# Memory feed-forward up projection: rounded features and remainders in one 512-column matmul, the two halves of the bank summed by ScalarE and VectorE

## The reference

```python
def swiglu(h, w_in, w_out):
    g, u = _split(h @ w_in, (D_FF, D_FF))
    return (jax.nn.silu(g) * u) @ w_out
...
        x = x + swiglu(rms_norm(x, norm_ffn[i]), ffn_w_in[i], ffn_w_out[i])
```

## Time and profile before

| | before |
|---|---|
| device time, median of 3 runs | 1661.8 us (1661.35 to 1661.95) |
| profiled execution: span from first to last instruction | 1659.6 us |
| its own time, with what lies around the span | not listed apart; the median lies 2.2 us over the span |
| granted TensorE clock, mean of the span | 0.998 of full |
| TensorE matmuls busy | 98% of the span |
| VectorE, ScalarE, GpSimd busy | 66%, 54%, 25% |
| DMA | 160 GB/s on average |

### The profile page before, as it was taken

How to read it: one execution, slowest core, us unless ns; L and a number is a source line. 1 busy time by engine, 2 the same in 40 slices (tenths; PEclk the granted TensorE clock), 3 DMA queues, 4 the chain that set the end, 5 groups by cost and what they waited for, 6 DMA issues and landing times. The chain is left out here.

```text
span 1659.6 us, 26949 instructions
## 1 busy us (share of the span) xinstructions
PE 1619.1 (98%) x10929; PEld 1462.8 (88%) x10929; DVE 1096.3 (66%) x1546; ACT 891.3 (54%) x1401; POOL 421.5 (25%) x460
## 2 busy tenths in 40 slices
PE   8999999999999999999999999999999999999999
PEld 7767899987887889998889998999888999999997
DVE  6875665645576665655577768777646876867763
ACT  6465554434455555443456746566445684756652
POOL 2500100002341120000147802244204690214430
PEclk9999999999999999999999999999999999999999
DMA  7523376556330236665555444766556444376652
GB/s 278 174 77 101 103 205 194 185 197 213 99 135 27 77 102 172 185 186 193 174 195 164 147 133 147 189 185 190 181 154 220 159 153 130 131 204 187 190 179 76
DMA packets 287067, 265.30 MB, mean 160 GB/s; under 512 B 12256, under 2 KB 247520, under 8 KB 286944
## 3 DMA queue, kind: packets, MB, share of 16 engines
q1 hardware_dynamic: 286944, 263.59, 50.8%
HBM read 262.52 MB, written 1.05 MB: 159 GB/s over the span
## 5 line engine op out<-in xcount | busy, mean ns | idle before, releaser
L144 DVE TENSOR_TENSOR w_lo<-w_raw,w_hi 128x2048 fp32r<-128x2048 f32 (+2 forms) x244 | 565.8, 2321 | 288.6 <-ACT w_hi L143 283.6
L143 ACT ACTIVATE w_hi<-w_raw 128x2048 fp32r<-128x2048 f32 (+2 forms) x244 | 462.9, 1902 | 214.6 <-PE bank L529 125.5
L1873 PE MATMUL bank<-h_hi,w_hi 128*128 128x256 f32 x1984 | 565.5, 285 | 4.7 <-issue 1.2
L1874 PE MATMUL bank<-h_lo,w_hi 128*128 128x256 f32 x1984 | 561.3, 283 | 0.0
L1875 PE MATMUL bank<-h_hi,w_lo 128*128 128x256 f32 x1984 | 561.2, 283 | 0.0
L1873 PEld LDWEIGHTS bank<-h_hi,w_hi 128*128 128x128 f32 x1984 | 380.5, 192 | 8.2 <-issue 7.5
L1874 PEld LDWEIGHTS bank<-h_lo,w_hi 128*128 128x128 f32 x1984 | 380.7, 192 | 0.1
L1875 PEld LDWEIGHTS bank<-h_hi,w_lo 128*128 128x128 f32 x1984 | 380.6, 192 | 0.0
L456 PE MATMUL bank<-w_hi,h_hi 128*128 128x512 f32 (+1 forms) x288 | 113.4, 394 | 5.4 <-DVE w_lo L144 3.3
L2953 POOL TENSOR_TENSOR cffn_hidden<-cffn_conv 128x256 f32<-128x256 f32 x44 | 73.7, 1675 | 155.5 <-ACT cffn_conv L2984 155.5
L457 PE MATMUL bank<-w_lo,h_hi 128*128 128x512 f32 (+1 forms) x288 | 111.9, 388 | 0.0
(11 more groups left out here) (447 smaller groups left out, 2858.0 us busy)
## 6 DMA issues: line engine op xcount, KB each, us to landing
w_raw<-in_w_in SPq DMA_DIRECT2D x48, 1024.0 KB, 5.0
w_raw<-in_ffn_w_in SPq DMA_DIRECT2D x88, 512.0 KB, 5.0
w_raw<-in_w_up SPq DMA_DIRECT2D x88, 512.0 KB, 5.2
w_raw<-in_ffn_w_out SPq DMA_DIRECT2D x22, 1024.0 KB, 4.9
w_raw<-in_w_down SPq DMA_DIRECT2D x22, 1024.0 KB, 5.0
w_raw<-in_nsa_w_in SPq DMA_DIRECT2D x10, 1024.0 KB, 5.2
w_raw<-in_mem_w_kv SPq DMA_DIRECT2D x8, 1024.0 KB, 5.1
w_raw<-in_w_branch SPq DMA_DIRECT2D x8, 1024.0 KB, 5.1
```

The costliest lines, as they stand in the source:

```text
L143: return act.activation(hi, raw, ACT.Copy)
L144: return dve.tensor_tensor(self.lo[:, cut_slot, 0:k * n], raw, hi.bitcast(F32), ALU.subtract)
L1873: pe.matmul(out, h, hi[:, f, :], start=(f == 0), stop=False)
L1874: pe.matmul(out, h, lo[:, f, :], start=False, stop=False)
```

## The change

`h_hi` and `h_lo` become the two halves of one tensor, so that one access pattern (`both`) reads the 256 columns of the rounded features and then the 256 of the remainders. `stationary_job` is replaced, in this stage only, by `summed_job`: for each feature tile one matmul of 512 columns (rounded weights by both parts, into a whole bank) and one of 256 columns (weight remainders by rounded features, into the bank's first half). A job now takes two banks, one for each tile, and two pairs of banks are used in turn. The gate tile signals `gate_done`, the up tile `w_used`. ScalarE copies the second half of each bank into SBUF (`rest`), VectorE adds it to the first half (`gate`, `upper`), and the multiplications that read the bank now read these buffers. TensorE waits before the gate tile of job j for the gate sum of job j - 2, and before the up tile for the up sum of job j - 2.

```diff
+def both(hi, lo):
+    return free(hi, [[lo.offset - hi.offset, 2], [1, hi.shape[-1]]])
...
-        self.h_hi, self.h_lo = self.keep("h_hi", [P, KD, S], F32R), self.keep("h_lo", [P, KD, S], F32R)
+        h = self.keep("h", [P, 2, KD, S], F32R)
+        self.h_hi, self.h_lo = h[:, 0, :, :], h[:, 1, :, :]
...
# ScalarE
+                def copy_rest(act, j, tile):
+                    act.wait_ge(*((gate_done, j + 1) if tile == 0 else (w.used, up[j] + 1)))
+                    if j >= 2:
+                        act.wait_ge(up_sum if tile else gate_sum, j - 1)
+                    act.activation(rest[:, j % 2, tile, :], k.bank[BANKS[2 * (j % 2) + tile]][:, S:2 * S], ACT.Copy)\
+                       .then_inc(up_rest if tile else gate_rest, 1)
+
                 for j in range(KF):
                     w.round_to(act, up[j] + 2)
+                    copy_rest(act, j, 0)
+                    if j >= 1:
+                        copy_rest(act, j - 1, 1)
                     act.wait_ge(opened, j + 1)
                     act.activation(gate[:, j % 2, :], gate[:, j % 2, :], ACT.Silu).then_inc(silu, 1)
                     if j >= 1:
                         act.wait_ge(prod, j)
                         act.activation(wide_hi[:, j - 1, :], hidden[:, (j - 1) % 2, :], ACT.Copy).then_inc(hid_hi, 1)
+                copy_rest(act, KF - 1, 1)
...
# VectorE
                 for j in range(KF + 1):
                     if j < KF:
                         w.cut_to(dve, up[j] + 2)
-                        dve.wait_ge(w.used, up[j] + 1)
+                        bank = k.bank[BANKS[2 * (j % 2)]]
+                        dve.wait_ge(gate_done, j + 1)
+                        if j >= 2:
+                            dve.wait_ge(prod, j - 1)
+                        dve.wait_ge(gate_rest, j + 1)
+                        dve.tensor_tensor(gate[:, j % 2, :], bank[:, 0:S], rest[:, j % 2, 0, :], ALU.add).then_inc(gate_sum, 1)
+                    if j >= 1:
+                        i = j - 1
+                        bank = k.bank[BANKS[2 * (i % 2) + 1]]
+                        dve.wait_ge(w.used, up[i] + 1)
+                        dve.wait_ge(up_rest, i + 1)
+                        dve.tensor_tensor(upper[:, i % 2, :], bank[:, 0:S], rest[:, i % 2, 1, :], ALU.add).then_inc(up_sum, 1)
+                    if j < KF:
                         if j == 0:
                             dve.wait_ge(row_factors.done, 1)
-                        dve.tensor_tensor(gate[:, j % 2, :], k.bank[BANKS[j % 4]][:, 0:S], row_factors.rows, ALU.mult)\
-                           .then_inc(opened, 1)
+                        dve.wait_ge(gate_sum, j + 1)
+                        dve.tensor_tensor(gate[:, j % 2, :], gate[:, j % 2, :], row_factors.rows, ALU.mult).then_inc(opened, 1)
                     if j >= 1:
-                        i = j - 1
                         dve.wait_ge(silu, i + 1)
+                        dve.wait_ge(up_sum, i + 1)
                         if i >= 2:
                             dve.wait_ge(hid_lo, i - 1)
-                        dve.tensor_tensor(hidden[:, i % 2, :], k.bank[BANKS[i % 4]][:, S:2 * S], gate[:, i % 2, :], ALU.mult)\
+                        dve.tensor_tensor(hidden[:, i % 2, :], upper[:, i % 2, :], gate[:, i % 2, :], ALU.mult)\
                            .then_inc(prod, 1)
...
# TensorE
-                    stationary_job(k, pe, up[j], k.bank[BANKS[j % 4]], rows_f, (prod, j - 3) if j >= 4 else None, j == 0)
+                    summed_job(k, pe, up[j], [k.bank[BANKS[2 * (j % 2) + tile]] for tile in range(2)], rows_f,
+                               ((gate_sum, j - 1), (up_sum, j - 1)) if j >= 2 else None, gate_done, j == 0)
...
+def summed_job(k, pe, c, banks, features, free_banks, tile_done, first=False):
+    w, hi, lo = k.weights, features.hi, features.lo
+    w.wait_cut(pe, c)
+    whi, wlo = w.halves(c)
+    for tile in range(2):
+        if free_banks is not None:
+            pe.wait_ge(*free_banks[tile])
+        bank = banks[tile]
+        for f in range(KD):
+            if tile == 0 and first:
+                features.wait_feature(pe, f)
+            h, l = whi[:, f, tile * P:(tile + 1) * P], wlo[:, f, tile * P:(tile + 1) * P]
+            pe.matmul(bank[:, :], h, both(hi[:, f, :], lo[:, f, :]), start=(f == 0), stop=False)
+            ins = pe.matmul(bank[:, 0:S], l, hi[:, f, :], start=False, stop=(f == KD - 1))
+        ins.then_inc(tile_done if tile == 0 else w.used, 1)
```

More of the change, by code:

```diff
@@ L1709, in block_memory_ffn @@
         cols = k.gains_1[:, (1 + 4 * layer) * KD:(4 + 4 * layer) * KD]
-        gate, hidden = k.small("gate", [P, 2, S]), k.small("hidden", [P, 2, S])
+        gate, upper = k.small("gate", [P, 2, S]), k.small("upper", [P, 2, S])
+        hidden, rest = k.small("hidden", [P, 2, S]), k.small("rest", [P, 2, 2, S])
         k.attention_buffers()
@@ L1725, in block_memory_ffn @@
         opened, silu, prod, hid_hi, hid_lo = s("opened"), s("silu"), s("prod"), s("hid_hi"), s("hid_lo")
+        gate_done, gate_sum, up_sum = s("gate_done"), s("gate_sum"), s("up_sum")
+        gate_rest, up_rest = s("gate_rest"), s("up_rest")
         k.ready()
```

## The result

The changed kernel takes 1672.05 us in the median of five runs (1671.36 to 1672.37), the kernel before 1661.79 (1660.71 to 1661.95). The ratio is 1.0063, 95% interval 1.0051 to 1.0075: slower by 10.3 us. Forecast: 1671.0, range 1667 to 1679. The profiled span is 1670.0 us (1659.6 before).

What follows compares the result with a forecast made beforehand. The prediction took the element-wise chain of ScalarE and VectorE to become the bound, at 5.907 us per turn: 4.6 us later per layer, 9.2 in all, span 1668.8, time 1671.0 us; range 1667 to 1679.

Steps and rivals of the forecast that it cites:

- the ring: In the 44 jobs, ScalarE and VectorE wait for each other in turn; grows from 5.247 to 5.907 us, becoming the bound.
- The price of the additions at their distance, not their duration: On VectorE between cut and scaled gate: two additions start 0.33 us apart, so the scaled gate comes 0.66 us later.
- The rival in which each addition costs 0.42 us: VectorE operations needing its own fresh result wait for their predecessor's end: turn 6.09 us, 1678.3 us in all; 10%.
- The start: Jobs 0 and 1: job 0 gets 0.15 us shorter; first rounding at 206.23, the next 5.37 us later at 211.60.
- Sum: Start, 19 turns of 5.907 us and last up tile put `down` 4.6 us later per layer, 9.2 in all.
- Two small terms that no row of before shows: At TensorE's up tiles: 0.06 us for the up sum's signal, 0.1 us for the restart after the last wait.
- Copies at nothing: ScalarE's two copies per job, right behind the rounding while VectorE cuts, cost nothing; uncovered, up to 0.66 us more.
- The third `down` chunk: At the start of `down`: cut by R(21) + 11.8, needed at R(21) + 12.8, R(21) being job 21's rounding; 1 us cover.
- TensorE's wait at job 2: Job 2's up tile could start at 214.2 but waits until 216.6 for the up sum: 2.4 us.
- The clock: Rival: TensorE's clock falls after job 2's wait, 1.6 us once, absorbed; in every job, 25 us per layer, 1720; 3%.
- TensorE gets 0.213 us shorter per job: In TensorE's jobs, a feature tile takes 346.7 ns instead of 360, so a job takes 5.55 us instead of 5.76.
- the rival on the other side: TensorE keeps the pace in the jobs: each layer ends them 4.7 us earlier, 1652.4 us in all; 6%.

Runs made afterwards that it cites:

- the kernel with the longer pause: Against the changed kernel reordered with the cut last: TensorE waits at job 2's up tile until VectorE has scaled job 2's gate; 1657.0 us, ratio 0.9977.

## Why the prediction was right

The time lies in the range because the mechanism was the forecast's own, the ring; the misses in its terms are small, all of one sign, and listed below.

- **The ring sets the pace: right.** Removing both additions brings the roundings back to 5.25 us apart, the third adds 0.33, and turning the order round frees TensorE. This is shown by the runs, not only by the sum.
- **Its length: right.** Forecast 5.907, measured 5.92 us. The 0.01 us makes 0.2 to 0.26 per layer (19 turns).
- **The price of the additions at their distance, not their duration: right.** The rival in which each addition costs 0.42 us falls: the starts are 0.33 apart in the changed kernel. The Trainium skill, page "VectorE: DVE Perf Modes", section "The DRAIN you can't avoid", has each operation wait until the pipe of the one before is empty, and adds that an operation which is not held starts earlier. The prediction took only the first half for its rival. For neighbours that do not depend on each other the trace agrees with the second half (starts 0.33 us apart at a duration of 0.42). Where the second waits for the first's result, the start comes 0.53 to 0.55 us after the first's, 0.20 to 0.22 more. The same section found that eight copies took the same time with a semaphore behind each and behind the last alone; it has no price for such a wait.
- **The start: small misses.** I priced that dependent pair, in the first iteration only, at 0.45 us; it is 0.53 (210.67 to 211.20 in layer 0). Job 0 got shorter by 0.06 us (5.93 against 5.99 from its first matmul to the transposes) instead of 0.15. Together 0.17 us a layer.
- **Sum.** Forecast +4.6 us per layer, counted from the first job; counted from L338 on, as the traces above are, that is +4.74, measured +5.15 and +5.04. Ring (0.26 and 0.19), dependent pair (0.09) and last tile (0.06 and 0.04) make up the difference. Forecast total 9.2, measured 10.3.
- **Two small terms that no row of before shows: right.** The 0.06 us for the signal and the 0.1 for the restart stand in the sum without a row. The changed kernel has 0.06 (from 246.49 to 246.55) and 0.10 (the matmul behind a late up tile comes 0.33 us after it, otherwise 0.23).
- **Copies at nothing: right** (twice the copies, same time). **The third `down` chunk: covered**, as forecast: cut at 342.30 in layer 0, asked for at 343.23. `down` ran on without a wait.
- **TensorE's wait at job 2: 1.97 us** of idle time on the profile; by starts the up tile comes 2.13 us later than it could, against 2.4 forecast, mostly since the tiles ahead of it ran at the slower pace. How long it is does not matter, as the ring sets when it ends. The forecast of 0.36 us per later job holds with the restart counted in: the up tiles start 0.16 to 0.29 us late, and 0.1 follows.
- **The clock: the rival was real, and priced rightly.** In the changed kernel's profile it stayed at 1.00, behind the wait at job 2 too. But the same wait was followed by 0.50 in one layer of three other kernels whose ring sets the pace, and cost them nothing, as the prediction had it ("loses 1.6 us once", taken up by the idle time); in the kernel with the longer pause, which has no such idle time, it cost 1.5 us. That the changed kernel's own profile shows no fall looks like chance. A fall in every job did not come: the windows show 1.00 with an up tile late in every turn, by 0.16 to 0.29 us there. So the warning of the Trainium skill, page "TensorE: Matmul & The Clock Gate", section "A second HAM failure mode: psum-queue depth-cycling", did not come true for these small idle times.
- **"TensorE gets 0.213 us shorter per job": too much.** This step carried the rival on the other side, not the forecast. The pair was priced at 0.3467 us, and the trace shows this in some stretches and 0.3533 in others. At the slower pace a job takes 5.65 us, and the saving is 0.11 instead of 0.21. So even with the ring broken the change brings 4.2 to 6.5 us, not 9.4.

## What to carry to other kernels

Busy shares do not show a ring: two engines at 52 and 66% (the first window above) can take turns so that their sum is the bound, and then every operation put between two handovers is paid in full, once per turn, while the same operation elsewhere is free (the copies). Measure the distance between two starts of the same step, sum the handovers around the ring, and compare this with the period of the engine that you want to relieve; here a margin of 0.51 us had to carry 0.66 more, against a job shortened by 0.21. Ask also how far back the new buffers make an engine wait: with two jobs instead of four, 2 of the 5 us per layer were lost at the first such wait. Before dropping such a change, look for the order in which prefetch work (rounding, cutting) stands behind the work that the result waits for; here it turned a loss of 10 us into a gain of 4.2 to 6.5.

## What the runs showed that I had not expected

- The same stream of alternating 512- and 256-column matmuls has two paces, 0.3533 and 0.3467 us per pair, at the same granted clock. It can differ between two layers of one execution. Over both layers it is worth up to 4.5 us, which would fit the scatter of kernels bound by TensorE (1656.4 to 1661.9 without sums), where kernels bound by the ring scatter by 1 to 2 us. This is not shown: each kernel has a trace of one execution only, and a fall of the clock, worth 1.5 us, would scatter the times as well.
- The granted clock fell to 0.50 for about 3 us behind four of ten waits of 1.79 to 2.53 us, and the other layer of the same execution kept 1.00 behind a nearly equal wait.
- On VectorE a dependent neighbour starts 0.53 to 0.55 us after its predecessor of 256 columns, an independent one 0.33.
